# Experts phase: a quarter of the down product ahead of h's second transposes, and six weight splits ahead of the first x

## The reference

```python
eid = (gsel[:, None] * EXPERTS_PER_GROUP + topi).reshape(-1)   # 2 of 32 experts per token
order = jnp.argsort(eid)
tok = order // TOP_K
sizes = jnp.bincount(eid, length=N_EXPERTS).astype(jnp.int32)
xs = xt[tok]
hgu = lax.ragged_dot(xs, w_gate_up, sizes)          # 1024 -> 2 x 512
g, u = jnp.split(hgu, 2, axis=-1)
ys = lax.ragged_dot(jax.nn.silu(g) * u, w_down, sizes)   # 512 -> 1024
ys = ys * wts.reshape(-1)[order][:, None].astype(ys.dtype)
out = jnp.zeros((t, dm), ys.dtype).at[tok].add(ys)
```

## Time and profile before

| | us |
|---|---|
| median of 3 runs | 3036.93 |
| lowest and highest | 3035.11 and 3037.29 |
| the profiled execution, its own time | 3050.11 |
| its span, first to last instruction | 3048.4 |
| TensorE matmuls busy | 2615.9 (86% of the span) |
| VectorE busy | 1682.2 (55%) |
| ScalarE busy | 1125.1 (37%) |
| GpSimd busy | 869.4 (29%) |
| VectorE low splits of expert weights (L1929), 288 | 422.8, mean 1514 ns |
| GpSimd low splits (L1929), 96 | 273.6, mean 2864 ns |
| ScalarE high splits (L2079), 384 | 377.6, mean 1055 ns |

### The profile page before, as it was taken

The page is one execution under the profiler, slowest core; times in us unless marked ns, Lnnn a source line. Parts: engine busy times, 40 slices in busy tenths (PEclk is TensorE's granted clock), DMA queues, the critical chain, the costliest instruction groups (busy, mean ns, idle before and its releaser), DMA issues. The chain is left out here.

```text
span 3048.4 us, 45654 instructions
## 1 busy us (share of the span) xinstructions
PE 2615.9 (86%) x14634; PEld 2258.8 (74%) x14635; DVE 1682.2 (55%) x3035; ACT 1125.1 (37%) x1906; POOL 869.4 (29%) x656
## 2 busy tenths in 40 slices
PE   1999996796997979968699998559999999999980
PEld 1888885685886868868578887348888888888870
DVE  5333333564665656648544543458576577557747
ACT  3111111343443434436311110247464466446633
POOL 2111111000000001024222232035455445445634
PEclk9999998898998989979899999779999999999995
DMA  4344444747465483348533331648688778768935
GB/s 159 125 147 141 155 144 145 198 146 195 145 185 175 138 220 128 126 123 210 169 123 125 130 133 75 216 145 321 223 303 282 220 258 298 230 224 300 342 103 234
DMA packets 277937, 568.47 MB, mean 186 GB/s; under 512 B 44624, under 2 KB 138960, under 8 KB 274768
## 3 DMA queue, kind: packets, MB, share of 16 engines
q1 hardware_dynamic: 186896, 430.90, 42.6%
q0 software_dynamic: 18752, 65.02, 8.5%
q10 hardware_dynamic: 72192, 71.31, 6.9%
HBM read 435.55 MB, written 131.60 MB: 186 GB/s over the span
## 5 line engine op out<-in xcount | busy, mean ns | idle before, releaser
L1929 DVE TENSOR_TENSOR e_wl<-rw_raw,e_wh 128x1024 fp32r<-128x1024 f32 (+1 forms) x288 | 422.8, 1514 | 25.8 <-ACT e_wh L2079 25.8
L2079 ACT ACTIVATE e_wh<-rw_raw 128x1024 fp32r<-128x1024 f32 (+1 forms) x384 | 377.6, 1055 | 4.2 <-PE e_py L2044 4.2
L1929 POOL TENSOR_TENSOR e_wl<-rw_raw,e_wh 128x1024 f32 (+1 forms) x96 | 273.6, 2864 | 72.3 <-ACT e_wh L2079 72.3
L301 PE MATMUL j_pg<-qkv_w_hi,j_xh 128*128 128x512 f32 (+1 forms) x640 | 242.3, 379 | 1.5 <-DVE j_xl L419 1.5
L303 PE MATMUL j_pg<-qkv_w_lo,j_xh 128*128 128x512 f32 (+1 forms) x640 | 237.1, 370 | 0.0
L302 PE MATMUL j_pg<-qkv_w_hi,j_xl 128*128 128x512 f32 (+1 forms) x640 | 236.1, 369 | 0.0
L999 POOL TENSOR_TENSOR b_o<-b_parts 128x128 f32<-128x128 f32 x64 | 31.0, 485 | 708.1 <-ACT b_parts L1116 708.1
L2030 PE MATMUL e_p_up<-e_wh,e_xh 128*128 128x256 f32 (+1 forms) x784 | 225.4, 288 | 0.0
L2031 PE MATMUL e_p_up<-e_wh,e_xl 128*128 128x256 f32 (+1 forms) x784 | 221.6, 283 | 0.0
L2032 PE MATMUL e_p_up<-e_wl,e_xh 128*128 128x256 f32 (+1 forms) x784 | 221.6, 283 | 0.0
L1050 PE MATMUL b_pg<-b_g_wh,b_g_xh 128*128 128x512 f32 x512 | 208.9, 408 | 5.0 <-DMA b_g_xl<-xt_lo 4.3
(11 more groups left out here) (340 smaller groups left out, 7158.8 us busy)
## 6 DMA issues: line engine op xcount, KB each, us to landing
rw_raw<-w_gate_up SPq DMA_DIRECT2D x256, 512.0 KB, 6.5
rw_raw<-w_down SPq DMA_DIRECT2D x128, 512.0 KB, 8.4
b_g_xh<-xt_hi SPq DMA_DIRECT2D x64, 512.0 KB
b_g_xl<-xt_lo SPq DMA_DIRECT2D x64, 512.0 KB
gates<-b_g_out ACTq DMA_DIRECT2D x64, 256.0 KB, 3.4
m_gt<-gates SPq DMA_DIRECT2D x16, 1024.0 KB
qk_hi<-j_qkh ACTq DMA_DIRECT2D x16, 832.0 KB, 4.5
qk_lo<-j_qkl ACTq DMA_DIRECT2D x16, 832.0 KB, 6.9
```

What stands on the lines that cost most here:

```text
L301: nc.tensor.matmul(out, xh[:, u, ks], w_hi[:, k, cs], start=(k == 0), stop=False)
L1929: (nc.gpsimd if done is w_lo_pool else nc.vector).tensor_tensor(wl[:, slot(e, s), :], raw[:, s:s + 1, :], f(wh[:, slot(e, s), :]), ALU.sub ...
L2079: nc.scalar.activation(wh[:, slot(e, s), :], raw[:, s:s + 1, :], ACT.Copy).then_inc(w_hi, 1)
```

## The change

Three orders are changed; no instruction is added or removed.

TensorE: `down` takes one step k at a time and waits for `h_lo` at steps 0 and 2. In a tile, step 0 now stands between `turn_x(g + 1, 0)` and `turn_h(g, 1)`, steps 1 and 2 behind `turn_h(g, 1)`, and step 3 behind `turn_x(g + 1, 1)`. The wait for `y_out` moves with step 0.

ScalarE: before the loops, the high splits of slots 0 to 5 of expert 0 stand ahead of the copies of the first x, the others behind.

VectorE: before the loops, the low splits of slots 0, 4 and 5 stand ahead of the two halves of the first `xl`, the others behind.

```diff
-            def down(g, e, p):
-                pe.wait_ge(h_lo, PIECES * g + p + 1)
-                for k in range(p * HP // P, (p + 1) * HP // P):
-                    wait_low(pe, e, KD + k)
-                    at, n = slice(k * P, (k + 1) * P), EARLY + KD + k
-                    for j in range(D // BANK):
-                        js = slice(j * BANK, (j + 1) * BANK)
-                        nc.tensor.matmul(py[:, js], hh[:, at], wh[:, n, js], start=(k == 0), stop=False)
-                        nc.tensor.matmul(py[:, js], hl[:, at], wh[:, n, js], start=False, stop=False)
-                        last = nc.tensor.matmul(py[:, js], hh[:, at], wl[:, n, js], start=False, stop=(k == KF - 1))
+            def down(g, e, k):
+                if k % (KF // PIECES) == 0:
+                    pe.wait_ge(h_lo, PIECES * g + k // (KF // PIECES) + 1)
+                wait_low(pe, e, KD + k)
+                at, n = slice(k * P, (k + 1) * P), EARLY + KD + k
+                for j in range(D // BANK):
+                    js = slice(j * BANK, (j + 1) * BANK)
+                    nc.tensor.matmul(py[:, js], hh[:, at], wh[:, n, js], start=(k == 0), stop=False)
+                    nc.tensor.matmul(py[:, js], hl[:, at], wh[:, n, js], start=False, stop=False)
+                    last = nc.tensor.matmul(py[:, js], hh[:, at], wl[:, n, js], start=False, stop=(k == KF - 1))
                 return last
...
                     pe.wait_ge(gathered, 16 * (g + 2))
                     turn_x(g + 1, 0)
-                    turn_h(g, 1)
 
                     pe.wait_ge(y_out, g + 1)
                     down(g, e, 0)
+                    turn_h(g, 1)
+                    down(g, e, 1)
+                    down(g, e, 2)
                     turn_x(g + 1, 1)
-                    down(g, e, 1).then_inc(down_done, 1)
+                    down(g, e, 3).then_inc(down_done, 1)
...
+            high(0, 0, range(LATE_X))
             high_x(0, 0)
             high_x(0, 1)
-            high(0, 0, range(NS))
+            high(0, 0, range(LATE_X, NS))
...
-            low_x(0, 0)
-            low_x(0, 1)
             for s in VECTOR_LOW:
+                if s == LATE_X:
+                    low_x(0, 0)
+                    low_x(0, 1)
                 low(dve, 0, s, w_lo)
```

## The result

The changed kernel took 3057.67 us (median of 20 runs; 19 of them 3031.82 to 3079.58, and one 6837.20, which nothing here explains) against 3036.9 us for the kernel before (20 runs, 3024.78 to 3046.45): a ratio of 1.0064, 95% interval 1.0045 to 1.0083. It is slower, by more than the 0.2% a measurement can tell, where 3030.3 was forecast, and it lies outside the range of 3018 to 3038. Without the one far off, its runs also spread over 48 us, those of the kernel before over 22.

A forecast was written before the change was run, and what follows sets the result against it. TensorE was taken to bound the experts, idle nearly only ahead of turn_h(g, 1). Terms -5.9 - 12.3 + 17.6 - 6.0 = -6.6 us, from the median 3036.93, gave 3030.3 us, range 3018 to 3038.

The forecast's parts named there:

- A: 18 tiles that wait in front of both VectorE products: the 0.33 us stall ahead of turn_h(g, 1) goes, -5.9 us.
- C: 16 first tiles that follow a one-tile expert, VectorE late: its loop gets 1.10 us longer each, +17.6 us.
- Quarter 2: Second quarter of the down product: needs the second half of hl, with margin 0.3 us, cost nothing.
- B: 15 tiles waiting before the first product only: VectorE splits slot 0 first, 14 gain 0.88 us each, -12.3 us.
- The first rival: GpSimd splits ahead of VectorE's slot 0 in B: +0.7 instead of -12.3 us, 3043.3 in all; chance 0.09.
- The start: First tile: the up product begins at 2029.4 instead of 2035.38 us, -6.0 us, bounds -4.5 and -7.5.
- the same: Outcome class for the whole kernel: no change that a measurement can tell, edge about 0.2%; chance 0.35.
- VectorE winning slot 0's turn in C: Rival in C: slot 0's split 2 us shorter, -14.4 instead of +17.6 us, 2998 in all; chance 0.08.
- Slower: Outcome class for the whole kernel, chance 0.12: GpSimd first in B 0.09, other losses of that size 0.03.
- the rule that was weighed: VectorE/GpSimd port pair: first to start holds it a whole instruction; if bandwidth is split, B gains 4.8 us, total 3037.8.

The follow-up runs named there:

- e5: Changed kernel with two empty semaphore instructions on GpSimd ahead of its split of slot 1; 3037.81 us, ratio 0.9990.
- e11: Changed kernel; VectorE waits for its split of slot 10, then two empty instructions, before slot 11's split; 3153.99 us (one run).
- e12: Old TensorE order, new start; VectorE waits for its split of slot 10, then four empty instructions, before slot 11's; 3100.81 us (one run).
- e6: Old TensorE order, new start, GpSimd waiting for VectorE's split of slot 11; 3015.03 us, ratio 0.9927 to the kernel before.
- e2: Kernel before with only TensorE's new order, old start kept; 3063.44 us, ratio 1.0077.
- e7: Changed kernel run again unaltered for another profile; 3074.31 us (one run).
- e8: Changed kernel run again unaltered for another profile; 3070.42 us (one run).
- e9: Changed kernel with three empty instructions on VectorE ahead of slot 11's split; 3055.45 us (one run).
- e10: Old TensorE order, new start, five empty instructions on VectorE ahead of slot 11's split; 3041.80 us (one run).

## Why the prediction was wrong, step by step

**A: right, a little dear.** The stall is gone in all 18. The gain is 0.27 per tile, not 0.33: the quarter apart from the others adds one more change from transposes to down matmuls, and the first matmul behind transposes holds back the next by 0.31 us where the usual distance is 0.23 (2750.85 to 2751.16 in tile 38, a C tile). 18 x -0.27 = -4.9, forecast -5.9. Quarter 2 never waited for `h_lo`.

**B: right, with its mechanism.** Slot 0's split was to come first and take some 1.2 us. One B tile after (it starts at 2354.41), VectorE, then GpSimd:

```profile
2363.36 1.22 DVE L1929 TENSOR_TENSOR e_wl<-rw_raw,e_wh 128x1024 f32 x1
2365.10 0.42 DVE L2138 TENSOR_TENSOR e_hl<-e_phh,e_hh 128x256 fp32r<-128x256 f32 x1 [0.52 <-ACT e_hh L2095]
...
2363.61 5.58 POOL L1929 TENSOR_TENSOR e_wl<-rw_raw,e_wh 128x1024 f32 x2 [1.53 <-ACT e_wh L2081]
```

VectorE asks 0.25 us ahead of GpSimd, where it was 0.39 behind the earlier trace rows, and its split takes 1.22 instead of 3.08. The first rival, GpSimd keeping its turn, did not happen. The gain is 0.72 per tile and not 0.88: 0.08 for the extra change as in A, and the gate product is 0.1 longer (mean 5.56 us, where A has 5.46 and both had 5.44 before): its first matmul is 0.33 us ahead of the second instead of 0.23. 14 x -0.72 = -10.1, forecast -12.3.

**C's loop: right, one term short.** TensorE waits ahead of `turn_h(g, 0)` and of the first quarter, and slot 0's split stays at 3.07, as said. The term was mis-sized: the loop grows by 1.28 us, not 1.10. The quarter was taken to start 0.05 behind `hl` and to take 1.43. In tile 38 `hl` ends at 2748.99, the quarter starts at 2749.22, 0.23 behind, and the transposes 1.49 behind that. The 0.05 came from a product and the transposes behind it; for the quarter the distance is 0.23. The gate product grew too, by 0.5 us (5.95 for 5.44) where the prediction had some 0.3; as it said, that costs nothing, because TensorE then waits for VectorE ahead of `turn_h(g, 0)`. 16 x 1.28 = +20.5, forecast +17.6.

**The start: right**, -5.0 for -6.0, inside its bounds.

Without a lost turn this adds up to -4.9 - 10.1 + 20.5 - 5.0 = +0.5 us, against -6.6. e5 is that case and has +0.5 (948.7 against 948.2). The terms alone would have moved the time to 3037, inside the range, and to "the same".

**The step that failed** is the sentence in C: "Here both queues move alike, so the turns stay: GpSimd stands waiting while VectorE is in slot 11's split, as now." They do not move alike. VectorE moved by 1.36 us and GpSimd by 1.14, because ScalarE had 0.21 us of slack ahead of the Silu. In the C tile of rows 8, before, ScalarE's Silu and the start of slot 11's split:

```profile
2851.58 0.60 ACT L2087 ACTIVATE e_act_g<-e_p_gate 128x512 f32<-128x512 f32 x1 [0.18 <-PE e_p_gate L2032]
...
2854.23 1.22 DVE L1929 TENSOR_TENSOR e_wl<-rw_raw,e_wh 128x1024 fp32r<-128x1024 f32 x1
```

After, the Silu of tile 38 follows ScalarE's work before it with no idle time:

```profile
2741.28 0.60 ACT L2089 ACTIVATE e_act_g<-e_p_gate 128x512 f32<-128x512 f32 x1
```

The prediction counted that slack in B ("0.23 before the Silu") and forgot it in C. Nor did it read by how much GpSimd was behind. The earlier trace rows has GpSimd at 2854.40; slot 11 is the last of the four splits from 2850.83 to 2855.45, so at about 1.13 each it begins near 2854.2 (in the trace 2854.23), and the margin was 0.2. The difference of two small numbers turned that 0.2 into -0.02. The three profiles of the unaltered kernel have 3, 6 and 7 lost turns, 5.7 us each; the 20.8 us between the medians are some 3 or 4 of them, and e5 gives them back by shifting GpSimd by 0.16 us. The spread of 48 us would fit as well, with nothing to eight lost turns, but that isn't shown: of those 20 executions only the profiled one, with 3, has a trace.

The rivals had a case for VectorE winning slot 0's turn in C, none for it losing slot 11's. "Slower" got 0.12, all of it for B and for unnamed losses.

What of the rule that was weighed, who starts first? The same split of slot 11 takes VectorE 1.21 us or 6.18, by who has the turn. The Trainium skill (SBUF — State Buffer, section "Who interferes with whom") says that the order of issue decides who blocks, and not the shape of the operation. The traces agree where the two are well apart: with GpSimd 0.13 us or more behind VectorE no turn was lost, with GpSimd 0.24 or more ahead all 29 were. They don't in the near ties, where GpSimd led and VectorE mostly got the turn. In tile 34 VectorE's split ends at 2668.85, 1.1 us behind the end of GpSimd's second split (2667.76): it waited for two instructions. The same page of the Trainium skill, section "SBUF: two separate sides", has the blocked engine wait for the one whole instruction of the other; here the measurement, two instructions, goes further, and it decides.

## What to carry to other kernels

When an edit delays two engines that share a turn, work out each one's shift by itself, with the slack of every engine between, and set the difference against the margin by which one asks ahead of the other now: here 0.2 us of margin decided 5.7 us in each tile that lost its turn. Here the near tie showed as one instruction with two durations far apart, and perhaps as the spread of the runs, so look at the longest of a group and not only its mean. Where the order matters, write it down with a semaphore: one wait on GpSimd brought the ratio from 1.0064 to 0.9931, and with it and the new start the kernel without TensorE's new order has 0.9927.

## What the runs showed of the hardware

**A turn lost early is lost twice.** In all profiles, I took GpSimd's back-to-back pairs of low splits and VectorE's low splits that were asked for during the first of a pair. The near ties that VectorE won are left to the next paragraph. Asked for 0.02 to 0.36 us behind its start, VectorE waited for both in the other 49 cases (5.7 to 6.2 us; 20 of the changed order, 16 of e11, 13 of e12), all of them slot 11's split. Asked for later, from 0.35 to 2.3 us behind it, it was served between the two, in all 238 (mostly 3.1 us, as in the earlier trace rows). Where the two ranges touch, at 0.35 to 0.36, both occur. Eight more, all in e6, were asked for 2.4 us behind it, some 0.04 ahead of the first split's end, and waited for the second as well. Why the early ones are passed over is open.

**The tie itself is not sharp.** In the near ties of the changed order (after, e2, e7, e8 and e9, 80 C tiles) GpSimd led by 0.01 to 0.04 us each time. VectorE still got the turn in 60, at leads up to 0.031, and lost it in 20, at leads from 0.022. No lead below 0.022 us took a turn.

**TensorE's clock.** A lost turn costs more than its 5 us. Stretches of tile 34, with busy us (count) of PE, PEld, DVE, ACT and POOL, granted clock, DMA share and GB/s:

```profile
2653.00:2665.00 12.00, 10.48 (x61) 8.72 (x60) 12.00 (x10) 10.24 (x11) 6.87 (x7) 1.00 1.00 376
2665.00:2669.00 4.00, 0.00 (x0) 0.00 (x0) 4.00 (x2) 0.00 (x0) 2.76 (x2) 0.89 1.03 296
2669.00:2673.00 4.00, 3.76 (x19) 3.76 (x19) 2.17 (x4) 0.39 (x1) 0.00 (x0) 0.50 0.89 279
2673.00:2680.00 7.00, 7.00 (x32) 5.71 (x31) 1.49 (x3) 2.42 (x4) 2.19 (x1) 0.86 0.52 195
```

TensorE stood for 5.76 us; then, in the stretch of 4 us from 2669, the granted clock is 0.50 (1.2 GHz), and a 256-column matmul follows the last after 0.21 us where it takes 0.12. The stalls of 0.8 and 1.2 us in tile 38 left the clock at 1.00 in the stretch that holds the second and in those on either side:

```profile
2746.00:2750.00 4.00, 2.78 (x21) 2.44 (x20) 3.31 (x3) 0.39 (x1) 4.00 (x2) 1.00 1.05 311
```

Against tile 38, the late transposes account for 5.0 us of tile 34's 6.1, the rest of the up product at the low clock for 1.3 and the first quarter for 0.9, while the wait ahead of that quarter (1.1) falls away.

**Empty semaphore instructions** cost GpSimd 0.08 us each where it waited for ScalarE ahead of them (e5), and VectorE nothing between two splits, three of them in e9 and five in e10.
